# A decoder step with PEER experts: the multiplier rows of the experts' dot products in PSUM instead of SBUF, the router's pieces in two PSUM banks

## What is computed

```python
q = (xb @ wq).reshape(PEER_BLOCK, PEER_HEADS, 2, PEER_DKEY // 2)      # 8 heads
s = jnp.einsum('thpd,pkd->thpk', q, subkeys)
s1, i1 = lax.top_k(s[:, :, 0], PEER_TOPK); s2, i2 = lax.top_k(s[:, :, 1], PEER_TOPK)   # 16 of 128, twice
cand = s1[..., :, None] + s2[..., None, :]                             # 256 sums
top_s, sel = lax.top_k(cand, PEER_TOPK)
idx = jnp.take_along_axis(cidx, sel, axis=-1)                          # 16 of 16384 experts
g = jax.nn.softmax(top_s, axis=-1)
act = jax.nn.gelu(jnp.einsum('thkd,td->thk', u_tab[idx], xb))
y = jnp.einsum('thk,thkd->td', g * act, v_tab[idx])
```

## Time and profile before

| | us |
|---|---|
| median of 3 timed runs | 2284.57 (2279.32 to 2291.11) |
| the profiled execution, its own time | 2296.89 |
| its span, from the first to the last record | 2295.1 |
| expert stage without the first tile: first u gather issued to last v gather issued | 957.6 to 2274.6 |
| TensorE's mean granted clock, share of full speed | 0.893 |

### The profile page before, as it was taken

One profiled execution on the slowest core, in us unless ns is written; L12 is line 12 of the kernel. 1 busy time (PEld: TensorE's weight loads), 2 busy tenths in 40 slices (PEclk: granted clock), 3 DMA queues, 4 the chain that ended last, 5 costly groups with the idle time before them and its releaser, 6 DMA issues.

```text
span 2295.1 us, 20759 instructions
## 1 busy us (share of the span) xinstructions
PE 1747.6 (76%) x4941; PEld 833.6 (36%) x4941; DVE 1210.8 (53%) x3126; ACT 481.3 (21%) x1213; POOL 1306.6 (57%) x1271
## 2 busy tenths in 40 slices
PE   6979899927581999977776777777767688788757
PEld 2425455612350444433332323333333344334322
DVE  2232556656776020056555655555646477668663
ACT  1222222201010222122211311211212122223221
POOL 2000101118756545667777777777767677777765
PEclk8989999868655999989999899899889799899889
DMA  8867587829968988899999999999999899999987
GB/s 285 305 247 249 189 291 235 293 92 376 331 200 290 412 311 315 322 338 348 348 359 339 322 342 335 342 339 366 324 323 323 315 335 355 323 361 336 346 304 263
DMA packets 237551, 713.21 MB, mean 311 GB/s; under 512 B 23101, under 2 KB 49055, under 8 KB 237456
## 3 DMA queue, kind: packets, MB, share of 16 engines
q0 software_dynamic: 156672, 570.49, 68.5%
q1 hardware_dynamic: 80488, 140.73, 17.3%
q10 hardware_dynamic: 312, 1.07, 0.1%
HBM read 704.42 MB, written 8.25 MB: 311 GB/s over the span
## 4 chain that ended last, share of the span: by engine, by line
issue 17%; PE 17%; POOL 14%; DMA 8%; DVE 7%; another core or an unknown queue 4%; ACT 2%; POOLq 1%; DVEq 0%; SPq 0%; ACTq 0%
PE ps_y L2290 15%; POOL u_rows L1877 7%; POOL v_rows L1883 6%; DMA v_rows<-in_peer_v_dram,v_idx 4%; DVE u_rows L2077 3%; DMA u_rows<-in_peer_u_dram,u_idx 3%; PE ps_r L2264 1%; ACT wt_diag L1982 1%; DMA v_rows<-in_peer_v_dram,tile_idx 1%; DVE key_scores_w L2088 0%; DMA subkeys<-in_peer_subkeys_dram 0%; DVE top_i L2090 0%; DVE top_i L2091 0%; DVE top L2089 0%
## 5 line engine op out<-in xcount | busy, mean ns | idle before, releaser
L2290 PE MATMUL ps_y<-v_rows,wt_diag 128*128 128x512 f32 x2176 | 1056.8, 630 | 253.1 <-DMA v_rows<-in_peer_v_dram,v_idx 147.5
L2290 PEld LDWEIGHTS ps_y<-v_rows,wt_diag 128*128 128x128 f32 x2176 | 414.0, 200 | 832.1 <-issue 788.0
L2077 DVE CUSTOM_DVE_ANT_0 u_rows<-u_rows,h_cur 128x1024 f32<-128x1024 f32 x416 | 494.0, 1225 | 311.7 <-DMA u_rows<-in_peer_u_dram,u_idx 293.5
L1877 POOL DMA_INDIRECT u_rows<-in_peer_u_dram,u_idx x416 | 463.9, 1115 | 186.1 <-issue 126.3
L1883 POOL DMA_INDIRECT v_rows<-in_peer_v_dram,v_idx x416 | 468.8, 1127 | 137.7 <-issue 117.6
L340 POOL DMA_INDIRECT low_rows<-in_peer_u_dram,tile_idx x128 | 183.1, 1431 | 220.9 <-DVE tile_dots L332 153.6
L606 PE MATMUL ps_z<-w_stream,hT 128*128 128x512 f32 (+5 forms) x560 | 244.3, 593 | 24.2 <-DVE hT L780 19.3
L1891 POOL DMA_INDIRECT v_rows<-in_peer_v_dram,tile_idx x128 | 122.8, 959 | 108.1 <-PE ps_y L2290 102.7
L332 DVE CUSTOM_DVE_ANT_0 low_rows<-low_rows,tile_rows 128x1024 f32<-128x1024 f32 x128 | 154.2, 1231 | 41.1 <-DMA low_rows<-in_peer_u_dram,tile_idx 40.1
L2087 DVE MAX8 top<-key_scores 128x8 f32<-128x128 f32 x64 | 18.2, 285 | 290.2 <-ACT key_scores L1973 198.1
L606 PEld LDWEIGHTS ps_z<-w_stream,hT 128*128 128x128 f32 (+1 forms) x560 | 99.3, 182 | 147.6 <-issue 112.6
(11 more groups left out here) (423 smaller groups left out, 1515.1 us busy)
## 6 DMA issues: line engine op xcount, KB each, us to landing
w_stream<-in_w_in_dram SPq DMA_DIRECT2D x25, 2048.0 KB, 9.4
w_stream<-in_ada_w_dram SPq DMA_DIRECT2D x12, 2048.0 KB, 13.4
w_stream<-in_peer_wq_dram SPq DMA_DIRECT2D x8, 1024.0 KB, 6.6
wq<-in_peer_wq_dram SPq DMA_DIRECT2D x4, 2048.0 KB, 42.9
w_stream<-in_w_in_dram SPq DMA_DIRECT2D x5, 1568.0 KB, 9.5
w_stream<-in_w_in_dram SPq DMA_DIRECT2D x5, 1536.0 KB, 13.8
u_rows<-in_peer_u_dram,u_idx POOLq DMA_INDIRECT x416
v_rows<-in_peer_v_dram,v_idx POOLq DMA_INDIRECT x416
```

What stands on the lines that cost most here:

```text
L1877: g.indirect_dma_start(u_rows[:, j, :], None, U, bass.IndirectOffsetOnAxis(where[:, j:j + 1], 0))\
L2077: v.tensor_tensor_reduce(u_rows[:, j, :], u_rows[:, j, :], h_cur[:, :], 1.0, 0.0, ALU.mult, ALU.add, dots[:, par, j:j + 1]).then_inc(s["u_ ...
L2290: mm = nc.tensor.matmul(ps_y[:, c * 512:(c + 1) * 512], diag[:, par, j, :], v_rows[:, j, c * 512:(c + 1) * 512], start=(first and j == 0), ...
```

## The change

1. `h_cur` becomes a PSUM tensor of 128 x 1024 floats, two banks (`ps_h_cur`). All 416 dots of `take_dots` now read one operand from SBUF (`u_rows`) and one from PSUM. The 128 dots of the first tile, in the mixers, stay as they are. `begin` copies from SBUF to PSUM.
2. A DMA can't write PSUM, so the sample's rows take a detour: SP's four DMAs go to a new SBUF tensor `h_spread`, and DVE copies it to `h_cur` before the sample's first dots. The DMAs now wait only for the sample's norm and stand ahead of the transfers of the sample's row numbers, not ahead of the last of them.
3. To free a bank, the scores share bank 0 with q (`ps_r` has 2 banks). PE's wait for ACT's copy of the scores of the head before moves from `head_scores` up into `head_q`.

```diff
-        h_cur = sb("h_cur", [P, D])
+        h_spread = sb("h_spread", [P, D])
...
-        ps_y, ps_h, ps_r = ps("ps_y", [P, D]), ps("ps_h", [P, KC, P]), ps("ps_r", [P, 3, 512])
+        h_cur = ps("ps_h_cur", [P, D])
+        ps_y, ps_h, ps_r = ps("ps_y", [P, D]), ps("ps_h", [P, KC, P]), ps("ps_r", [P, 2, 512])
...
+                sp.wait_ge(s["h_normed"], LT + 1)
+                for i in range(QS):
+                    sp.dma_start(h_spread[i * NS:(i + 1) * NS, :], h_next[0:NS, :]).then_inc(s["hs_in"], 16)
                 for g in range(SG):
-                    if g == SG - 1:
-                        sp.wait_ge(s["u_used"], NG * NB)
-                        for i in range(QS):
-                            sp.dma_start(h_cur[i * NS:(i + 1) * NS, :], h_next[0:NS, :]).then_inc(s["hs_in"], 16)
...
-                    a(sc[:, :, :], ps_r[:, 2, 0:256], ACT.Copy).then_inc(s["sc_out"], 1)
+                    a(sc[:, :, :], ps_r[:, 0, 256:512], ACT.Copy).then_inc(s["sc_out"], 1)
...
                 dve.wait_ge(s["hs_in"], 16 * QS)
+                v.tensor_copy(h_cur[:, :], h_spread[:, :]).then_inc(s["copied"], 1)
+                dve.wait_ge(s["copied"], LT + 1)
...
                 def head_q(H, h):
 
+                    if not isinstance(H, int) or H:
+                        hold(pe, s["sc_out"], H)
...
                     hold(pe, s["qt_out"], H + 1)
-                    if not isinstance(H, int) or H:
-                        hold(pe, s["sc_out"], H)
                     for k in range(2):
-                        mm = nc.tensor.matmul(ps_r[:, 2, k * PK:(k + 1) * PK], qT[:, k, :], subT[:, k, :], start=True, stop=True)
+                        mm = nc.tensor.matmul(ps_r[:, 0, 256 + k * PK:256 + (k + 1) * PK], qT[:, k, :], subT[:, k, :], start=True, stop=True)
```

## The result

The changed kernel is slower, by 1.1%: little, but clear of the scatter. In interleaved runs on one chip it took 2313.18 us in the median of 20 (2295.09 to 2322.89), the kernel before 2288.14 us in the median of 20 (2268.11 to 2312.13): ratio 1.011, 95% interval 1.0085 to 1.0134. Forecast were 2157 us and a range of 2130 to 2225.

The account below looks back on a forecast made before the run. POOL's issue stream was taken as the bound: 155 us won from gathers and row-number copies less 27 us given back, other parts 0, makes 128 us less than the median 2284.6, so 2157 us; range 2130 to 2225.

Parts of the forecast that it names:

- What bounds the kernel: Stage from 957.6 to 2274.6 us: POOL's issue stream sets its end, 1281 of 1317 us; gathers under dots lose 142 us.
- The hold goes, the dot costs the same: Dots reading PSUM no longer delay POOL's gathers and row-number copies, 155 us less; a dot stays at 1225 ns.
- What is late next: Per group after the change: POOL 21.25 us, DVE 15.6 (21.4 in the last tile), PE 18.8, transfers 20.7.
- What is given back: Losses against the gain from stops, tied groups, DVE's copy, last v gathers and transfers: 27 us, bounds 10 and 60.
- about nine stops, a fixed time, 15 us: At tile boundaries and in the last tile ACT stops up to 10.4 us; POOL loses 1.5 to 2 us each, 15 us.
- the 0.5 us per tied group: In the last tile, ten groups where DVE and POOL need about equal time lose some 0.5 us each.
- the 4 us for transfers: Gather transfers running near their limit give back 4 us of the gain.
- The last sign named in the prediction: It is wrong if POOL's waits at tile boundaries grow to several times 9 us.
- Part 2 and part 3: SP's moved DMAs cost 0; PE's moved wait in head_q costs 0 to 10 us, taken as 0.
- the transfers take over: Rival, chance 0.15: DMA engines hold no more than 362 GB/s, 23.2 us per group, 2198 us.
- the hold stays: Rival, chance 0.10: dots delay POOL's gathers for another reason, such as the product written to SBUF; 2284 to 2290 us.
- The slower end: Rival, chance 0.03: dots with a PSUM input take two passes, 2.3 us, and become the bound; 2335 us.

Follow-up runs that it names:

- pace_d: Changed kernel with a GpSimd fill of 256 scratch elements per partition behind every gather of the expert stage: 2264.55 us, ratio 0.9839 to the kernel before.
- before_d: Kernel before the change with a GpSimd fill of 256 scratch elements per partition behind every gather: 2427.03 us, ratio 1.0574 to the kernel before.
- part3: Kernel before with only the scores moved into q's bank and PE's wait moved up into head_q: 2299.38 us, ratio 0.9987.
- parts12: Changed kernel with q's own bank back, scores in the bank of q's transposes and PE's wait ahead of those transposes: 2312.04 us, ratio 1.0114.
- half_after: Changed kernel with gathers of half rows, 2 KB instead of 4 KB per row: 2321.21 us, ratio 1.0111 to the kernel before.
- pace_e5: Repeat run of the changed kernel with a fill of 192 scratch elements per partition behind every gather: 2246.21 us, ratio 0.9784 to the kernel before.

## Why the prediction was wrong

- *What bounds the kernel*: right. The kernel before is paced by POOL's stream, and the hold costs what was said: with late increments out of the way (pace_d against before_d) the change is worth about 160 us.
- *The hold goes, the dot costs the same*: right, by its numbers. 1115 and 1127 ns became 959 and 940 (forecast about 945), the dot went from 1225 to 1217, and gathers and copies take 155.6 us less where 155 were counted. The Trainium skill's first sentence there (page "SBUF — State Buffer", section "Who interferes with whom"), that two SBUF inputs contend with a GpSimd instruction that reads SBUF, agrees with the traces: in after 322 gathers start under a dot, which now has one SBUF input, and they take 0.94 us in the mean and none over 0.98. Its inference that a `tensor_tensor` spares the writing of descriptors does not: the gather of 1450.04 started under one with two SBUF inputs and took 1.69 us.
- *What is late next*: this is where it failed. It asked each engine for its busy time per group and found room everywhere: PE 18.8 of 21.25 us. None was the bound. A hand-over of PE was: q, 2.6 to 14.4 us late in the loops wherever the trace has it, with two more hand-overs behind it ahead of DVE's keys, which no busy time shows. The group takes 25.6 us and not 21 to 22. GB/s stayed at 335 in place of 380.
- *What is given back*: the term "about nine stops, a fixed time, 15 us" is the step that was mis-sized. The 10.41 us stop marked remote in the earlier trace rows was read as something from outside that comes about nine times and is at most that long. The trace of before has more: 25 such waits ahead of ACT's three copies, up to 16.2 us, 157.1 us in all, in the middle of tiles too. By the runs on the pace they are PE's increments held back while gathers come 1.24 us apart without a break, something that the change itself makes the rule by taking away many of the held gathers that broke the rows. In place of 27 us 172 were given back in the idle time ahead of the gathers, and the stage became 13 us longer. Two other terms are too small beside this to be read from the traces: the 0.5 us per tied group and the 4 us for transfers. The last sign named in the prediction, POOL's waits growing to several times 9 us, is the one that came: 9.0 to 40.8 on remote, 28.4 to 160.7 on dots.
- *Part 2 and part 3*: part 3 costs 0, as said (part3 0.9987, parts12 the same loss as after). For part 2 only the trace speaks, and it agrees: the copy on DVE takes 1.22 us and the transfers are long done by then.
- *Rivals*: none of the four describes what happened. That the transfers take over is refuted by half_after. That the hold stays is refuted by the gathers' means, 959 and 940. The slower end had the wrong mechanism, a dearer dot.

## What to carry to other kernels

An idle time that the profile marks as remote, in a kernel on one core, is a question and not a constant: look at which increment it waited for, when the instruction that gives it was recorded, and what ran in between, since a faster neighbour may make it common. When a stream of gathers becomes faster, count the hand-overs from TensorE that stand in a row on the path and not only the engines' busy time. And where such a stream runs at its full pace, try it somewhat slower: here 0.14 us more between gathers turned a loss of 1.1% into a gain of 2.2% (1.8 to 2.5% by pace_e5).

## What was not expected of the hardware

While GpSimd issues indirect gathers back to back at 1.24 us, TensorE's semaphore increments reach the others late, those of q mostly by 13 to 14 us, in the end several at 0.06 us from each other. At 1.33 us they come singly, 1.5 to 11.9 us late, at 1.41 and 1.43 us mostly on time in the loops; at 1.72 us, with TensorE busy 50.00 of 50 us, all 27 recorded came after 0.02 us. In the changed kernel half the bytes per gather changes nothing (167 against 335 GB/s), nor do half of the increments of used rows; in pace_d neither do 3.7 more landing updates per us from another queue. ACT waited up to 13.7 us for q in after. The Trainium skill has a warning that comes near (page "VectorE: DVE Perf Modes", section "The TRN2 errata — SBUF-src ops pay a fixed extra latency per instruction"): increments at a high rate from one engine can deadlock another, and kernels with dense increments from several engines should space them. Whether what is seen here is the same is not shown: nothing deadlocked, spacing the gathers helped, and thinning TensorE's increments did not.
